# Decoder step on one core: the low weight parts of 24 MLP blocks a layer come from an adding DMA instead of VectorE

## The reference

```
def sq_relu_mlp(h, w_up, w_down):
    return jnp.square(jax.nn.relu(h @ w_up)) @ w_down

xp = xp + rmsnorm(sq_relu_mlp(rmsnorm(xp, norm_pre_mlp[i]), mlp_w_up[i], mlp_w_down[i]), norm_post_mlp[i])
```

## Time and profile before

| | us |
|---|---|
| median of 3 runs (lowest, highest) | 1403.37 (1403.0, 1404.66) |
| the profiled execution | 1399.53 |
| its span, first to last instruction | 1397.9 |
| TensorE matmul busy | 1346.0 (96%) |
| VectorE busy | 883.5 (63%) |
| ScalarE busy | 597.0 (43%) |
| GpSimd busy | 217.7 (16%) |

### The profile page before, as it was taken

The page is one execution under the profiler, slowest core; times in us unless marked ns, Lnnn a source line. Parts: engine busy times, 40 slices in busy tenths (PEclk is TensorE's granted clock), DMA queues, the critical chain, the costliest instruction groups (busy, mean ns, idle before and its releaser), DMA issues.

```text
span 1397.9 us, 28131 instructions
## 1 busy us (share of the span) xinstructions
PE 1346.0 (96%) x11193; PEld 1240.4 (89%) x11193; DVE 883.5 (63%) x1574; ACT 597.0 (43%) x1099; POOL 217.7 (16%) x228
## 2 busy tenths in 40 slices
PE   7999997999999999999999999999999999999997
PEld 7656665699999999999988888899999999999996
DVE  5457786437786786874366544544678678687435
ACT  5356662325533434433345433343454343443322
POOL 2220024021130230310210000001203013031011
PEclk9999998999999999999999999999999999999999
DMA  9400023231332323332314233233232333333321
GB/s 257 127 9 1 1 67 88 85 91 46 107 91 83 99 61 106 101 91 86 93 55 140 61 110 110 76 96 90 61 105 63 106 86 82 105 95 93 98 62 65
DMA packets 203921, 120.55 MB, mean 86 GB/s; under 512 B 13990, under 2 KB 199616, under 8 KB 203808
## 3 DMA queue, kind: packets, MB, share of 16 engines
q1 hardware_dynamic: 197776, 104.74, 27.0%
q0 software_dynamic: 6032, 14.24, 3.2%
HBM read 111.37 MB, written 7.59 MB: 85 GB/s over the span
## 4 chain that ended last, share of the span: by engine, by line
PE 77%; DVE 12%; ACT 5%; issue 4%; SPq 1%; DMA 0%; DVEq 0%; ACTq 0%
PE ps L2278 35%; PE ps L2779 16%; PE ps L2340 5%; PE ps L2752 4%; PE ps L2348 2%; PE ps L2516 2%; DVE y L1586 1%; PE ps L2497 1%; PE ps L2611 1%; PE ps L2549 1%; DVE ps L1744 1%; SPq L759 1%; PE ps L2302 1%; PE ps L2698 1%; PE ps L2532 1%
## 5 line engine op out<-in xcount | busy, mean ns | idle before, releaser
L2278 PE MATMUL ps<-act_hi,w_hi 128*128 128x280 f32 (+1 forms) x1408 | 296.3, 292 | 2.2 <-DVE act_lo L1848 0.9
L2278 PE MATMUL ps<-act_hi,w_lo 128*128 128x280 f32 (+1 forms) x1408 | 294.1, 290 | 0.0
L2278 PE MATMUL ps<-act_lo,w_hi 128*128 128x280 f32 (+1 forms) x1408 | 293.2, 289 | 0.0
L2278 PEld LDWEIGHTS ps<-act_hi,w_hi 128*128 128x128 f32 x1408 | 222.0, 188 | 8.3 <-issue 6.4
L2278 PEld LDWEIGHTS ps<-act_hi,w_lo 128*128 128x128 f32 x1408 | 222.9, 188 | 0.0
L2278 PEld LDWEIGHTS ps<-act_lo,w_hi 128*128 128x128 f32 x1408 | 221.9, 188 | 0.0
L2779 PE MATMUL ps<-h_hi,w_hi 128*128 128x280 f32 (+1 forms) x672 | 197.1, 293 | 5.5 <-DVE w_lo L1891 3.1
L2779 PE MATMUL ps<-h_lo,w_hi 128*128 128x280 f32 (+1 forms) x672 | 196.4, 292 | 0.0
L2779 PE MATMUL ps<-h_hi,w_lo 128*128 128x280 f32 (+1 forms) x672 | 196.2, 292 | 0.0
L998 ACT CAST w_hi<-w_raw 128x1024 fp32r<-128x1024 f32 x76 | 79.4, 1048 | 168.8 <-PE ps L2278 122.4
L2779 PEld LDWEIGHTS ps<-h_hi,w_hi 128*128 128x128 f32 x672 | 128.0, 190 | 7.3 <-DVE w_lo L1891 3.5
(11 more groups left out here) (365 smaller groups left out, 2579.0 us busy)
## 6 DMA issues: line engine op xcount, KB each, us to landing
w_raw<-in_mlp_w_up_dram SPq DMA_DIRECT2D x64, 512.0 KB, 4.1
w_raw<-in_mlp_w_down_dram SPq DMA_DIRECT2D x40, 512.0 KB, 4.2
w_pair<-in_mlp_w_down_dram SPq DMA_DIRECT2D x24, 512.0 KB, 5.5
w_raw<-in_gla_w_in_dram SPq DMA_DIRECT2D x24, 512.0 KB, 3.8
pg_ckv<-in_cache_ckv_dram SPq DMA_DIRECT2D x64, 128.0 KB, 2.4
w_raw<-in_mla_w_o_dram SPq DMA_DIRECT2D x8, 512.0 KB, 5.0
sts<-in_state_gla_dram POOLq DMA_DIRECT2D x4, 1024.0 KB, 6.6
out_dram<-sts POOLq DMA_DIRECT2D x4, 1024.0 KB, 5.2
```

The lines of the kernel that those rows point to most:

```text
L2278: last = nc.tensor.matmul(out[:, h, 0:n], w[:, c, :], a[:, c, t0 + n * h:t0 + n * h + n], start=(c == 0 and k == 0), stop=(c == DC - 1 and ...
```

## The change

For 24 up blocks a layer (blocks 4 to 7 of quarter 0, all of quarters 1 and 2, blocks 0 to 3 of quarter 3; `summed`) the low part is made without VectorE. ScalarE writes the high part as before and then, in a second instruction, minus the rounded value into `w_lo`. GpSimd then issues a DMA that reads the same raw block from DRAM once more and adds it onto `w_lo` in place (`sum_up`). TensorE waits for that transfer on a semaphore of its own, `w_summed`. VectorE only raises `w_split` where the subtraction stood, so that the counts of all others hold; SyncE's loads wait for ScalarE's count `w_rounded` instead where the block before was a summed one. GpSimd's MLP is written out for its three quarters instead of a loop. Three semaphores of small loads become one (`gate_in`).

```
+def summed(q, k):
+
+    return 0 <= k < 8 and 4 <= 8 * q + k < 8 * CROSSED + 4
...
+        def sum_count(layer, q, k):
+            return 16 * ((layer * CROSSED * 8 + q * 8 + k - 4) // 2 + 1)
...
-                        sp.wait_ge(w_split, q * Q_GROUPS + (g0 + k - RAW + 1))
+                        sp.wait_ge(w_rounded if summed(q, k - RAW) else w_split, q * Q_GROUPS + (g0 + k - RAW + 1))
...
                     if i == 0:
-                        sp.wait_ge(w_split, q * Q_GROUPS + (g0 + 6 + k + 1))
+                        sp.wait_ge(w_rounded, q * Q_GROUPS + (g0 + 6 + k + 1))
...
+            def sum_up(layer, q, k):
+
+                g = G_MLP[layer] + q * Q_GROUPS + k
+                pool.wait_ge(w_rounded, g + 1)
+                if layer or 8 * q + k >= 6:
+                    pool.wait_ge(w_summed[k % 2], sum_count(layer, q, k) - 16)
+                pool.dma_start(w_lo[slot(g)][:], cols(mlp_w_up[layer], q * D + k * P), accum_op=ALU.add)\
+                    .then_inc(w_summed[k % 2], 16)
...
-                for i in range(Q_PAIRS):
-                    weight_forms(layer, 0, i)
-                with pool.Fori(1, CROSSED) as q:
+                for q in range(CROSSED):
+                    for k in range(4, 8):
+                        sum_up(layer, q, k)
                     for i in range(Q_PAIRS):
                         weight_forms(layer, q, i)
+                    for k in range(4):
+                        sum_up(layer, q + 1, k)
...
-                nc.scalar.copy(w_hi[slot(G_MLP[layer] + k)][:], w_raw[k % RAW][:]).then_inc(w_rounded, 1)
+                w = slot(G_MLP[layer] + k)
+                nc.scalar.copy(w_hi[w][:], w_raw[k % RAW][:])
+                nc.scalar.activation(w_lo[w][:], w_raw[k % RAW][:], ACT.Copy, scale=-1.0).then_inc(w_rounded, 1)
...
             def split_up(layer, q, k):
...
-                nc.vector.tensor_tensor(w_lo[w][:], w_raw[k % RAW][:], w_hi[w][:].bitcast(F32), ALU.subtract).then_inc(w_split, 1)
+                dve.sem_inc(w_split, 1)
...
-                pe.wait_ge(w_split, q * Q_GROUPS + (g + 1))
+                if summed(q if isinstance(q, int) else 1, k):
+                    pe.wait_ge(w_summed[k % 2], q * 64 + sum_count(layer, 0, k))
+                else:
+                    pe.wait_ge(w_split, q * Q_GROUPS + (g + 1))
```

More of the change, by code:

```diff
@@ L550, in trunk @@
         ident = cst[:, C_ID:C_ID + P]
-        const_in = sem("const_in")
+        gate_in = sem("gate_in")
         mconst_in = sem("mconst_in")
@@ L657, in trunk @@
         so_placed = sem("so_placed")
-        gd_in = sem("gd_in")
+        w_summed = [sem(f"w_summed{i}") for i in range(2)]
         turn_mm = sem("turn_mm")
@@ L662, in trunk @@
         pads_zeroed = sem("pads_zeroed")
-        wg_in = sem("wg_in")
         gla_step = sem("gla_step")
@@ L890, in weight_forms @@
                 g = G_MLP[layer] + (cross_group(i - 1, 0) if i else cross_group(Q_PAIRS - 1, 0) - Q_GROUPS)
-                later = i or not isinstance(q, int)
+                later = i or q
                 wait_pair(pool, layer, q, i, 0)
@@ L918, in _ @@
             pool.dma_start(uv[:], uv_v).then_inc(uv_in, 16)
-            pool.dma_start(cst[:, P:N_GLA_CONST], const[:, P:N_GLA_CONST]).then_inc(const_in, 16)
+            pool.dma_start(cst[:, P:N_GLA_CONST], const[:, P:N_GLA_CONST]).then_inc(gate_in, 16)
             pool.wait_ge(kpe_ready, 4)
@@ L951, in _ @@
             pool.wait_ge(h_ready, 32)
-            pool.dma_start(gd_raw[:], gla_w_in[0].rearrange("(c p) m -> p c m", p=P)[:, :, 3 * D:]).then_inc(gd_in, 16)
-            pool.dma_start(wg[:], gla_w_gate[0]).then_inc(wg_in, 16)
+            pool.dma_start(gd_raw[:], gla_w_in[0].rearrange("(c p) m -> p c m", p=P)[:, :, 3 * D:]).then_inc(gate_in, 16)
+            pool.dma_start(wg[:], gla_w_gate[0]).then_inc(gate_in, 16)
             add_squares(N_POST_MLP0)
@@ L1872, in split_up @@
             def split_up(layer, q, k):
-                w = slot(G_MLP[layer] + k)
-                dve.wait_ge(w_rounded, q * Q_GROUPS + (G_MLP[layer] + k + 1))
-                nc.vector.tensor_tensor(w_lo[w][:], w_raw[k % RAW][:], w_hi[w][:].bitcast(F32), ALU.subtract).then_inc(w_split, 1)
+                dve.sem_inc(w_split, 1)
             def split_pair(layer, q, i, s):
@@ L2168, in sample_states @@
                 last.then_inc(st_ready, 1)
-            dve.wait_ge(gd_in, 16)
+            dve.wait_ge(gate_in, 16 * 3)
             nc.vector.tensor_tensor(gd_w[:], gd_raw[:], gain[:, R_PRE_MIX + DC:R_PRE_MIX + 2 * DC].rearrange("p (c o) -> p c o", o=1)
@@ L2855, in gate @@
                     pe.wait_ge(blk_read, R_OF["gd"] + 1)
-                    pe.wait_ge(wg_in, 16)
+                    pe.wait_ge(gate_in, 16 * 3)
                 pair_free(f"G{h}")
```

## The result

The changed kernel takes **1451.0 us** (median of 4 runs, 1449.5 to 1452.8) against 1403.4 (1403.0 to 1404.7) for the kernel before: a ratio of 1.0342, 95% interval [1.0325, 1.0358]. The profiled execution took 1449.5 us with a span of 1447.8, 49.9 more than the span before. The forecast was 1433 with a range of 1404 to 1455: direction and range held, but the loss is 47.6 us where 29.4 were forecast, and 1451 lies above the 1425 to 1446 of the main case.

The account below looks back on a forecast made before the run. TensorE was taken as the bound, waiting 4.4 us for VectorE's side at first pairs. Relief -7.2, quarter-end waits +18.0, block-4 waits +7.4 and clock +11.2 sum to +29.4 on 1403.4: 1432.8, say 1433; range 1404 to 1455.

Parts of the forecast that it names:

- main case: Whole kernel: transfer wait L of 5.8 to 8.5 us, with half-rate clock after waits, 1425 to 1446 us; chance 65%.
- What bounds the kernel: Both MLPs: TensorE, 96% busy, waits for VectorE's side at quarter 0's first pair, 4.4 us together.
- Minus 7.2, the backlog is gone: Quarter 0, both layers: VectorE's lateness vanishes, saving 4.4 us of first-pair waits and 2.8 us of clock.
- 0.9 gained in each of four steps: Quarter 0, blocks 0 to 3: ScalarE's two instructions beside VectorE's eviction shorten each step from 3.0 to 2.1 us, 3.6 in all.
- the backlog stays: Rival, quarter 0: ScalarE sets the pace and 7.2 us are not gained; given little, put into the range.
- The eight places, and their slack: TensorE waits at block 0 after six quarter ends (3.8 us left for L) and block 4 of quarter 0, twice (3.1).
- L = 6.8: Time from ScalarE's second instruction to TensorE's start: 6.5 us for the transfer plus 0.3 for GpSimd's start.
- The bounds, 4.1 to 8.5: Limits for L: a plain load, 3.8 + 0.3 us, and two plain loads one after the other, 8.2 + 0.3.
- The clock, 8 x 1.4: After each of eight TensorE waits of 3 us or more, half rate costs 1.4 us: 11.2 us more.
- the add is slow: Rival at the adding DMA: L of 8.5 to 12 us, giving 1446 to 1474 us; chance 12%.
- short wait: Rival: L of 4.9 to 5.8 us, six waits of 1.1 to 2.0, 1406 to 1414 us; chance 10%.
- Hidden, and faster: Rival at block 0 after six quarter ends: transfer hidden, kernel faster if L is below 4.2 us; chance 8%.

Follow-up runs that it names:

- no_negate: Changed kernel without the adding DMAs and without ScalarE's second instruction; low parts of 48 blocks not formed: 1397.3 us, ratio 0.9948.
- no_transfer: Changed kernel without the adding DMAs, ScalarE's second instruction kept, TensorE waiting for ScalarE's count (low parts wrong): 1401.2 us, ratio 0.9988.
- low_last: Changed kernel, but TensorE does the 32 high-part matmuls first and waits for the sum only before the 16 low-part ones: 1408.9 us, ratio 1.0037.
- no_short_low_last: Changed kernel with the eight short-slack blocks split on VectorE and low-part matmuls last in the other 40: 1404.4 us, ratio 1.0003.
- plain_copy: Changed kernel with GpSimd's DMAs as plain copies into `w_lo` instead of adds (low parts wrong): 1422.7 us, ratio 1.0132.
- half_sum: Changed kernel with the adding DMA covering only four of each block's eight chunks (other half wrong): 1418.8 us, ratio 1.0098.

## Why the prediction was right and wrong, point by point

- **What bounds the kernel**: right. TensorE waited for VectorE only at the first pairs, 4.4 us. `no_negate`, which takes all 48 subtractions away, gains 6.9 us: the waits and the clock behind them.
- **"Minus 7.2, the backlog is gone"**: the size of the prize was right, the mechanism was wrong. The step that failed is "0.9 gained in each of four steps": with ScalarE's second instruction in place the first two steps lost 0.75 us together, the next two gained 2.2, slow forms beside GpSimd took 0.7 back, and 0.7 us were gained in all. `no_transfer` came out 2.5 us below the kernel before, not 7.2. In the changed kernel the waits at the first pair do vanish, because TensorE itself is late by 4.7 us at block 4; with the same order of VectorE they are back in each run where it is held for less than 1 us at blocks 4 and 5 (`no_transfer`, `low_last`, `no_short_low_last`). The prediction named this among its rivals (*the backlog stays*), and gave it little for just that reason. So the term has the right sum for a partly wrong cause, and that part is luck.
- **The eight places, and their slack**: right. The waits stand at block 4 of quarter 0 and block 0 of quarters 1 to 3 in both layers, and nowhere else. The slack is 3.2 to 3.4 and 3.9 to 4.2, where 3.1 and 3.8 were read from the kernel before.
- **L = 6.8**: this is the term that was mis-sized. L measures 8.2 in the mean, 1.4 more, of which the larger slack takes 0.2 back. Taking the prediction's slacks, the 34.5 us of waits are a mean L of (34.5 + 6 x 3.8 + 2 x 3.1) / 8 = 7.9. Either way it is 34.5 us of waits for 25.4, 9.1 us of the 18.2 between forecast and result. The bounds, 4.1 to 8.5, held for the mean and for seven of the eight (the eighth is 8.8). The choice inside them went by the 6.5 of two loads at once. What it missed is that a plain copy by GpSimd already takes 6.0, 1.8 more than one by SyncE (`plain_copy`), so that doubling starts from a higher floor. GpSimd's own 1 MB loads took 6.1; I read that as the price of twice the bytes, where 1.6 to 2.7 us of it were the time to the first packet.
- **The clock, 8 x 1.4**: right in kind, short in size. Each of the eight waits is followed by half rate, two of them for 6.8 us. The kernel has ten stretches of 3.4 us for eight, and the MLPs have 13.3 us beyond the waits where the prediction has 8.4 net of the two that went. That is 4.9 of the 18.2. The other 4.2 us of the difference I can't place: they lie outside the two MLPs or in what differs between executions.
- **The time against the cases**: with L below 8.5 the main case was to give 1425 to 1446. It gave 1451, in the band of *the add is slow*, because of the longer stretches of half rate and the 4.2 us outside the MLPs, not because L was that long.
- **GpSimd**: its instruction takes 1.55 us, not 0.92. The 0.92 was a plain copy's (`gd_raw`, 1024 pieces as well, but of 64 B), and `plain_copy` has 0.87; the add is what is longer. It cost nothing that shows: the first packet comes after 2.7 us with the add and after 2.6 without, and TensorE waits for none of GpSimd's forms.
- **The rivals**: *short wait* is what `half_sum` and `plain_copy` show (waits of 1.5 to 2.7, where the prediction had 1.1 to 2.0; 1419 and 1423 us). The prediction's 1406 to 1414 for it was low, because of these longer waits and because four of them in the first kernel and three in the second were followed by half rate. *Hidden, and faster* is `no_short_low_last`: hidden, and not faster (1404.4). *The add is slow* began at 8.5; the mean L of 8.2 came near it; single transfers took up to 12.4 us to land, where TensorE did not wait for them.

## What to carry to other kernels

Work taken off an engine that isn't the bound is worth what the bound waits for it, and no more: here 4.4 us of waits and 2.8 of clock, whatever the 58.8 us of busy time. Before it is moved to a DMA, find the shortest time between the moment a buffer comes free and the moment it is wanted (here 5 to 6 us at eight of 48 places), and lay the whole new chain into it: 2.1 + 8. If the bound engine can take another operand first, the same chain may nearly fit (34.5 us of waits became 7.0 by an order of matmuls). And a backlog that stems from two engines handing work back and forth could here be shortened by the order of one of them alone, for 0.3% of the time.
